# Decoder step: low parts of the weights over the loaded chunk, four places for the high parts, another order of the value pages in SP's queue

## What is computed

```python
q, k, v, u = split(rms_norm(x) @ w_in)          # 2048 -> 5120; q, k normed by head
o = (softmax(q1 k1) - lam * softmax(q2 k2)) v   # 8 heads; past keys, values: 16 pages a sequence
c = silu(layer_norm(depthwise_conv31(glu(u))))
x = x + [rms_norm(o); c] @ w_out                # 2048 -> 2048
y = x + relu(rms_norm(x) @ w_up)**2 @ w_down    # 2048 -> 8192 -> 2048
```

## Time and profile before

| what | us |
|---|---|
| median of 3 runs (1700.35 to 1705.51) | 1704.58 |
| the profiled execution's own time | 1703.94 |
| its span in the trace | 1702.2 |
| PE busy, share of the span | 1550.0 (91%) |
| DVE busy | 988.1 (58%) |
| ACT busy | 620.5 (36%) |
| span of visits 1 to 4 (67.7 to 212.9) | 145.2 |
| span of visits 5 to 9 (212.9 to 529.8) | 316.9 |
| w_out and feed-forward (about 765 on) | 937 |

### The profile page before, as it was taken

One profiled execution on the slowest core, in us unless ns is written; L12 is line 12 of the kernel. 1 busy time (PEld: TensorE's weight loads), 2 busy tenths in 40 slices (PEclk: granted clock), 3 DMA queues, 4 the chain that ended last, 5 costly groups with the idle time before them and its releaser, 6 DMA issues.

```text
span 1702.2 us, 32371 instructions
## 1 busy us (share of the span) xinstructions
PE 1550.0 (91%) x11299; PEld 1381.3 (81%) x11299; DVE 988.1 (58%) x1483; ACT 620.5 (36%) x948; POOL 420.7 (25%) x654
## 2 busy tenths in 40 slices
PE   6999887898887877779999999999999999999998
PEld 4988765565565544439999999999999999999998
DVE  3587756998998575524455454455445454445444
ACT  4433222122123344414354433344334343344433
POOL 4893546756776444100000000000000000000000
PEclk9999999988988777779999999999999999999999
DMA  6746689999999565564445544555545555455453
GB/s 180 230 129 179 206 287 333 348 310 318 346 314 353 157 195 184 158 237 135 150 149 162 166 166 162 170 162 166 168 162 168 163 165 167 161 167 165 163 169 130
DMA packets 163844, 340.50 MB, mean 200 GB/s; under 512 B 33915, under 2 KB 33971, under 8 KB 163168
## 3 DMA queue, kind: packets, MB, share of 16 engines
q1 hardware_dynamic: 120592, 267.29, 48.8%
q0 software_dynamic: 43168, 72.15, 13.8%
HBM read 334.00 MB, written 5.96 MB: 200 GB/s over the span
## 4 chain that ended last, share of the span: by engine, by line
PE 75%; DVE 8%; issue 6%; DMA 6%; ACT 3%; POOL 1%; POOLq 1%; SPq 0%; ACTq 0%; DVEq 0%
PE acc L586 21%; PE acc L588 21%; PE acc L587 21%; DMA v_page<-in_cache_v 3%; DMA k_page<-in_cache_k 2%; DVE conv L1468 2%; PE aux L659 2%; PE acc L808 1%; DVE w_lo L1330 1%; DVE k_page L1402 1%; PE aux L683 1%; PE aux L717 1%; PE acc L604 1%; PE acc L830 1%; POOL k_page L493 1%
## 5 line engine op out<-in xcount | busy, mean ns | idle before, releaser
L1330 DVE TENSOR_TENSOR w_lo<-raw,w_hi 128x1024 fp32r<-128x1024 f32 x368 | 451.0, 1226 | 523.3 <-ACT w_hi L989 522.4
L989 ACT CAST w_hi<-raw 128x1024 fp32r<-128x1024 f32 x368 | 385.9, 1049 | 723.0 <-PE acc L588 723.0
L586 PE MATMUL acc<-a_hi,w_hi 128*128 128x288 f32 (+1 forms) x1920 | 593.4, 309 | 35.1 <-DVE w_lo L1330 23.2
L587 PE MATMUL acc<-a_lo,w_hi 128*128 128x288 f32 (+1 forms) x1920 | 580.0, 302 | 0.0
L588 PE MATMUL acc<-a_hi,w_lo 128*128 128x288 f32 (+1 forms) x1920 | 579.8, 302 | 0.0
L586 PEld LDWEIGHTS acc<-a_hi,w_hi 128*128 128x128 f32 x1920 | 369.7, 193 | 80.0 <-issue 43.7
L493 POOL DMA_DIRECT2D k_page<-in_cache_k x512 | 332.2, 649 | 257.0 <-PE aux L659 134.1
L587 PEld LDWEIGHTS acc<-a_lo,w_hi 128*128 128x128 f32 x1920 | 370.2, 193 | 0.5
L588 PEld LDWEIGHTS acc<-a_hi,w_lo 128*128 128x128 f32 x1920 | 370.1, 193 | 0.0
L588 PE MATMUL acc<-h_hi,w_lo 128*128 128x288 f32 x1024 | 302.2, 295 | 0.0
L587 PE MATMUL acc<-h_lo,w_hi 128*128 128x288 f32 x1024 | 301.5, 294 | 0.0
(11 more groups left out here) (217 smaller groups left out, 1006.3 us busy)
## 6 DMA issues: line engine op xcount, KB each, us to landing
k_page<-in_cache_k POOLq DMA_DIRECT2D x512, 128.0 KB, 6.2
v_page<-in_cache_v SPq DMA_DIRECT2D x128, 512.0 KB, 8.3
raw<-in_w_up SPq DMA_DIRECT2D x128, 512.0 KB, 3.7
raw<-in_w_down SPq DMA_DIRECT2D x128, 512.0 KB, 3.7
raw<-in_w_in SPq DMA_DIRECT2D x80, 512.0 KB, 5.6
raw<-in_w_out SPq DMA_DIRECT2D x32, 512.0 KB, 3.7
x_nat<-in_x_prompt SPq DMA_DIRECT2D x3, 1024.0 KB, 9.0
out<-y_nat SPq DMA_DIRECT2D x8, 256.0 KB, 2.7
```

Source lines behind the costliest of these rows:

```text
L586: mm(out, wh, ah, start=(kt == 0), stop=False)
L587: mm(out, wh, al, start=False, stop=False)
L989: nc.scalar.copy(w_hi[:, j % SPL], raw[:, j % RAW]).then_inc(hi_ok, 1)
L1330: v.tensor_tensor(w_lo[:, j % SPL], raw[:, j % RAW], w_hi[:, j % SPL].bitcast(F32), ALU.subtract)\
```

## The change

The low part of a chunk is written over the loaded chunk: `w_lo` lies on the same memory as `raw`, and `w_hi` gets four places (the memory in all stays the same). `hi` and `lo` no longer wait for PE; a load does. SP waits for PE's use of the chunk four earlier: on `w_used`, and for j = 3 on `acc_ok` of the visit before. In `body`, SP now queues value page j + 2 at step j, and at the steps 14 and 15 pages 0 and 1 of the next sequence, each ahead of the chunk of weights of that step. One wait on `w_used` is added in ACT's `operands` (the last visit of w_out), where the wait in `free` had covered the reuse of a_hi.

```diff
-        raw = sb("raw", [P, RAW, CK, VC])
-        w_hi = sb("w_hi", [P, SPL, CK, VC], F32R)
-        w_lo = sb("w_lo", [P, SPL, CK, VC], F32R)
+        (raw,), (w_lo,) = aliased(
+            [("raw", [P, RAW, CK, VC], F32)],
+            [("w_lo", [P, RAW, CK, VC], F32R)])
+        w_hi = sb("w_hi", [P, RAW, CK, VC], F32R)
...
             def load_w(n, j, src):
-                sp.wait_ge(lo_ok, NC * n + j + 1)
+                if j == RAW - 1:
+                    if not isinstance(n, int) or n:
+                        sp.wait_ge(acc_ok, MT * n)
+                elif j >= RAW:
+                    sp.wait_ge(w_used, (NC - 1) * n + j - RAW + 1)
+                elif not isinstance(n, int) or n:
+                    sp.wait_ge(w_used, (NC - 1) * (n - 1) + NC - RAW + j + 1)
                 sp.dma_start(raw[:, j % RAW], src).then_inc(raw_in[j % RAW], 16)
...
-            def body(vs, n=None, nxt=None):
-                for j in range(N_PAGES + 2):
-                    if vs is not None and j >= 2:
-                        load_values(vs, j - 2)
-                    if n is not None and j % 2 == 1 and j < N_PAGES:
+            def body(vs, n=None, nxt=None, last=False):
+                for j in range(N_PAGES):
+                    if j + 2 < N_PAGES:
+                        if vs is not None:
+                            load_values(vs, j + 2)
+                    elif not last:
+                        load_values(0 if vs is None else vs + 1, j + 2 - N_PAGES)
+                    if n is not None and j % 2:
                         c = (j - 1) // 2 + RAW
                         if c < NC:
                             load_w(n, c, w_src(n, c))
...
-                slot = kt // CK % SPL
+                slot = kt // CK % RAW
...
-        def free(eng, n, j):
-            if j == 1:
-                eng.wait_ge(acc_ok, MT * n)
-            else:
-                eng.wait_ge(w_used, (NC - 1) * n + max(j - 1, 0))
...
             def hi(n, j):
                 act.wait_ge(raw_in[j % RAW], 16 * (NC // RAW * n + j // RAW + 1))
-                free(act, n, j)
-                nc.scalar.copy(w_hi[:, j % SPL], raw[:, j % RAW]).then_inc(hi_ok, 1)
+                nc.scalar.copy(w_hi[:, j % RAW], raw[:, j % RAW]).then_inc(hi_ok, 1)
...
             def operands(j):
+                act.wait_ge(w_used, (NC - 1) * (MLP_V0 - 1) + j - 1)
...
             def lo(n, j):
                 dve.wait_ge(hi_ok, NC * n + j + 1)
-                free(dve, n, j)
-                v.tensor_tensor(w_lo[:, j % SPL], raw[:, j % RAW], w_hi[:, j % SPL].bitcast(F32), ALU.subtract)\
+                v.tensor_tensor(w_lo[:, j % RAW], raw[:, j % RAW], w_hi[:, j % RAW].bitcast(F32), ALU.subtract)\
                     .then_inc(lo_ok, 1)
```

More of the change, by code:

```diff
@@ L40 @@
 RAW = 4
-SPL = 2
 VR = 4
@@ L391, in _ @@
                 body(s)
-            body(N_SEQ - 1)
+            body(N_SEQ - 1, last=True)
             sp.wait_ge(sc_mm, NG * N_SEQ)
```

## The result

The changed kernel takes 1692.99 us, the median of 10 runs, against 1704.68 for the kernel before on the same chip: a ratio of 0.9936, 95% interval 0.9917 to 0.9955. One execution of e11 took 2123.35 us at a granted clock of 0.648 and is left out of its ratio and of every mean here. So it is faster by 0.4 to 0.6%, 7 to 11 us; 15.6 were forecast. The profiled execution has a span of 1691.0 us, 11.2 less than before.

What follows compares the result with a forecast made beforehand. PE, 91% busy, was taken as the bound, held up early by the wait in `free`, with value pages queued behind chunks. 1703.94 - 10.5 - 3.1 - 2 = 1688.3 us, 1689.0 on the runs' scale; range 1681 to 1700.

Steps and rivals of the forecast that it cites:

- Starts of visits 2 to 4 and the clock: Early visits: PE's late starts shrink by 2.65, 1.9, 0.7 and 1.2 us, and 3.1 us of low clock go.
- The upper end: Early visits: 10.5 us gained if the square roots on ACT come earlier too; the range was 5.3 to 10.5.
- hidden by 0.8 us at the worst: Visits 1 to 4: later loads have 10.1 us of lead against a need of 8.4, at longest 9.3.
- Start of visit 5: PE's wait of 1.60 us keeps 0.7 for emptying a bank, so 0.9 us are gained.
- Value pages in visit 5: End of visit 5: page 14 is queued 4.7 us earlier, saving DVE 3.1 us, with 0 as the other end.
- Value pages in visits 6 to 9: Four bodies: pages queued earlier gain 2 us in all, range 0 to 7.6.
- I take 0.5 each, 2 us: Bodies of visits 6 to 9: the gain taken for earlier value pages, near the lower end of 0 to 7.6 us.
- slower: Rival, chance 0.08: earlier value pages delay keys by 3.2 us in each of five bodies, 16.2 us, giving 1710.
- The order as a separate gain: Value pages queued earlier on SP were priced as their own terms, 3.1 us in visit 5 and 2 in later bodies.
- The cost 0: Loads that now wait for PE's use of the chunk four earlier stay hidden and cost nothing; from above 3.7 us.
- Loads in the last stage, the tail: Last stage: loads need 6.5 us (longest 7.7) of a 9.5 us lead, 1.8 to 3 to spare, cost 0.

Runs made afterwards that it cites:

- e11: The changed kernel run once more, unaltered, beside the kernel before: 1693.66 us, ratio 0.9937.
- e3: The changed kernel with the old wait for PE's use of the chunk two earlier put back in `hi` and `lo`: 1705.92 us, ratio 1.0025.
- e5: The changed kernel run once more, unaltered, beside the kernel before: 1694.89 us, ratio 0.9957.
- e2: The kernel before with only the new order of the value pages: 1705.94 us, ratio 1.0039.
- e8: The changed kernel with the last 15 of 31 convolution taps made on 2 of 256 columns, less DVE work: 1688.24 us, ratio 0.9918.
- e9: The changed kernel with only half of each value page loaded and that half used twice: 1667.29 us, ratio 0.9791.
- e1: The changed kernel with the old order of the value pages in SP's queue: 1877.45 us, ratio 1.1027.
- e6: The changed kernel with weight loads in loops waiting for PE's use of one chunk more: 1728.81 us, ratio 1.0161.
- e4: The changed kernel with matmuls without use ahead of PE's wait for `o_rows` in visits 5 to 9: 1687.70 us, ratio 0.9933.

## Why the prediction held, and which terms did not

**Starts of visits 2 to 4 and the clock: right.** The forecast was 9.6 us (2.65 + 1.9 + 0.7 + 1.2 and 3.1 of clock); the stretch gained 10.5, 8.2 and 10.1 in three profiles, and e3 lost it again. The idle times came out at 1.21 and 0.94 instead of 1.0 and 0.7, the one in visit 4 at 5.21 instead of 5.3, and the clock stayed up behind the first two. The upper end was nearer than the lower, since the chain through the square roots did move. Its weak spot was named too high: "hidden by 0.8 us at the worst". In e5 the chunk 3 of visit 1 landed late enough that ACT waited 3.43 us, and visit 2 started 2.06 us late and with the old clock loss (timelines of ACT and PE, and the window behind):

```profile
74.50 1.04 ACT L991 CAST w_hi<-raw 128x1024 fp32r<-128x1024 f32 x1 [3.43 <-DMA raw<-in_w_in]
```
```profile
98.49 0.41 PE L597 MATMUL acc<-a_hi,w_hi 128*128 128x304 f32 x1 [2.06 <-DVE z L1339]
```
```profile
98.45:103.45 5.00, 4.96 (x24) 4.96 (x25) 3.78 (x5) 4.78 (x8) 4.61 (x6) 0.66 0.22 85
```

The step compared a landing with PE's need. Here the landing is needed sooner, by the square roots that stand behind the conversion on ACT.

One reading of the clock was off: the mean of 0.66 is not always a stretch that begins at the lower level. Behind the 2.57 us of the kernel before, the first 0.89 us run at 1.00, and the half speed (0.50, 1.2 GHz) comes after that (windows; e5 above has the same, 0.98 over the first 0.95 us and then 0.50 over 3 us):

```profile
133.11:134.00 0.89, 0.89 (x6) 0.89 (x7) 0.89 (x3) 0.89 (x3) 0.00 (x0) 1.00 0.01 2
```
```profile
134.50:137.50 3.00, 3.00 (x14) 3.00 (x14) 0.74 (x1) 0.10 (x1) 0.00 (x0) 0.50 0.27 56
```

The price, about 1.5 us, stays as it was read.

**Start of visit 5: mis-sized.** 0.9 us were booked, with the 0.7 for a bank kept. The first chunk of visit 5 takes 7.9 us (7.3 and 8.2 in the repeats) instead of 11.0: 2.8 to 3.7. The whole wait of 1.60 is gone, and the clock behind it is better. Windows of that chunk, before and after:

```profile
212.90:223.90 11.00, 6.78 (x34) 6.24 (x35) 7.30 (x19) 5.83 (x13) 2.59 (x4) 0.81 0.99 345
```
```profile
201.50:209.40 7.90, 5.42 (x35) 5.02 (x34) 5.27 (x13) 3.68 (x12) 2.60 (x4) 0.90 1.04 354
```

In e2 and e3 it is 11.0 again: this too comes from `free`.

**Value pages in visit 5: right in size.** 3.1 were forecast. From the end of the first chunk to `o_rows`, before 56.5 us, the changed kernel 54.1, 53.2 and 54.2: 2.3 to 3.3, of which e2, with the order alone, has 1.9. And `o_rows` follows there without idle time, where DVE had waited 3.13 us (timeline of DVE):

```profile
263.07 0.41 DVE L1530 COPY o_rows<-aux 128x256 f32<-128x256 f32 x1
```

**Value pages in visits 6 to 9: wrong.** The step that failed is "I take 0.5 each, 2 us". The bodies lost 2.0 to 6.6 us, and 4.1 in e2. The range of that term ended at 0, although the row that was quoted, DVE without idle time ahead of `o_rows`, said that PE's waits for pages bought nothing. DVE ends these bodies, so their length is what stands in DVE's own row: its work and its waits. The window from o_rows to o_rows before (the changed kernel's stands with e8 and e9), and DVE's waits in it for PE's transposes, before and after:

```profile
280.40:537.50 257.10, 212.36 (x1636) 148.77 (x1636) 240.15 (x453) 58.55 (x95) 173.15 (x268) 0.90 0.99 329
```
```profile
DVE pT L1494 <- PE aux L683: 7.2, 3, 3.8
```
```profile
DVE pT L1496 <- PE aux L694: 7.0, 3, 3.3
```

DVE's work is 240.2 us before and 241.6 to 241.8 after. Its waits for keys grew from 6.4 us to 11.0 (11.4 and 9.1 in the repeats, 11.2 in e2), its waits for PE's transposes did not grow (7.2, then 7.0, 3.2, 4.9, and 4.5 in e2). So what grew is the keys' wait, by 2.7 to 5.0 us, and DVE's work, by about 1.5; the reason of the latter is open. The rival *slower* had the mechanism of the keys, with 3.2 us a body; it came to about 1 us a body, enough to turn the sign of this term, too little for that of the whole. PE's waits for pages became one of 6 to 8 us for `o_rows`, with a lower clock behind it, but that wait is not in DVE's row: the clock as a cause of this loss is not shown.

The Trainium skill ("DMA: Bandwidth & Descriptors", "Queues, rings and completion order") has each DMA engine take turns between the queues it has work for. By that rule, as the prediction read it, a longer queue of SP costs the keys nothing. The traces agree with the small size, not with zero: with the order alone changed (e2) the keys' median landing is 8.5 us instead of 7.1. No run here shows the turns.

**The order as a separate gain: wrong.** The prediction priced the order of the pages as a term of its own, and the wait of the loads at 0 with pages "behind a load wait". e1 shows that the two belong together: without the new order, the loads' wait costs some 180 us. The cost 0 held only because the order was changed with it.

**Loads in the last stage, the tail: right.** PE stays at 800 of 800 us. The need was put at 6.5 us and is 6.0, by e6. The smallest slack, 0.4 us, is less than the 1.8 to 3 that the prediction left.

Together: 9.6 + 0.9 + 3.1 + 2 were forecast; 8.2 to 10.5, 2.8 to 3.7, 2.3 to 3.3 and -2.0 to -6.6 were measured. So by luck the start of visit 5, booked too small, covered part of a later term that turned out a loss, and the sum, 15.6, came out 5 to 8 us above the measured 7 to 11.

**Open.** The stretch behind visit 9 differs by 5 to 6 us between executions of the same code (1163.4 and 1169.3 in the repeats), and runs of one kernel scatter by 10 us; no run here looked for the cause. The difference lies between the ends of the visits 9 and 10 (262.5, 262.1 and 268.3 us in the changed kernel's three profiles), with the prompt's attention in it; all that comes behind takes 909 in each. Nor do the runs settle what the lower clock behind the wait for `o_rows` costs, if anything: 3.2 us, give or take 2.7, in one comparison, nothing by ratio in another.

## What to carry to other kernels

Follow an idle time back past the engine that it names: here PE waited for emptied banks, DVE for a conversion, and the conversion for PE itself, and two places more for the converted chunk freed the whole ring. When a wait is moved to another event, look at what stands behind it in the same queue, since a queue's order that was free may then be a condition. And before pricing a removed wait in a stage, ask which resource is full there: take away a part of each in turn (bytes, work) and see whose waits grow.

## What the runs showed of the hardware

Behind an idle time of PE of 2.06 us the next 24 matmuls ran at a mean granted clock of 0.66, 4.96 us, as behind 2.57 and 3.67 (4.89 and 4.96); behind 1.39, 1.21 and 0.94 it stayed at 1.00. Behind 2.06 and 2.57 the fall came late: PE ran on at 0.98 and 1.00 for 0.9 us, and then at 0.50. Matmuls without use, into a bank that nobody reads, held it up: 34 of them in visit 4 took the mean over 24 us from 0.86 to 1.00, and the visits 1 to 4 from 134.7 to 132.9 us. Where PE's clock was low, the DMA engines moved less: at the start of visit 9, with the same order of loads, 218 GB/s at a clock of 0.65 and 267 at 0.87 (e4). That their places come free later is the likely reason, not one that a run shows by itself.

The order of one queue shows in another: with value pages queued earlier on SP's queue, key pages from POOL's queue landed after 8.5 us (median, e2) instead of 7.1, and with half the bytes of the values after 4.8 (e9).
